# The second block's modulation: from TensorE in the delta rule to VectorE beside the first two perceptrons

## The reference, cut to what matters

```
def ada_params(cvec, w_ada, b_ada):
    return jnp.split(jax.nn.silu(cvec) @ w_ada + b_ada, N_ADA, axis=-1)
...
    for l in range(DEPTH_2):
        last = l == DEPTH_2 - 1
        sa, ca, ga, sm, cm, gm = ada_params(c_lat, w_ada[l], b_ada[l])
        sa_c, ca_c, ga_c, sm_c, cm_c, gm_c = ada_params(c_cx, w_ada[l], b_ada[l])
        ...
        h = modulate(rms_norm_2(x, g_mix[l]), sa, ca)
        hc = modulate(rms_norm_2(ctx, g_mix[l]), sa_c, ca_c)
```

## Time and profile before

| | us |
|---|---|
| median of 3 runs (2899.91 to 2905.57) | 2902.4 |
| the profiled execution, its own time | 2905.16 |
| its span, first to last instruction | 2903.4 |
| TensorE busy | 2716.3 (94%) |
| VectorE busy | 1439.0 (50%) |
| ScalarE busy | 887.6 (31%) |
| GpSimd busy | 88.5 (3%) |
| delta stage, about | 371 to 798 |
| first perceptron, start, about | 1020 |

### The profile page before, as it was taken

One profiled execution on the slowest core, in us unless ns is written; L12 is line 12 of the kernel. 1 busy time (PEld: TensorE's weight loads), 2 busy tenths in 40 slices (PEclk: granted clock), 3 DMA queues, 4 the chain that ended last, 5 costly groups with the idle time before them and its releaser, 6 DMA issues.

```text
span 2903.4 us, 48524 instructions
## 1 busy us (share of the span) xinstructions
PE 2716.3 (94%) x20932; PEld 2174.1 (75%) x20932; DVE 1439.0 (50%) x2470; ACT 887.6 (31%) x1508; POOL 88.5 (3%) x141
## 2 busy tenths in 40 slices
PE   6899988888899999999899899999999899899998
PEld 4677565667878788877777678888888776688876
DVE  3455555668853454434366654333334456544434
ACT  3344411100032333223345433222222345333322
POOL 0000011112200000000000000000000000000000
PEclk9999999999999999999999999999999999999999
DMA  6100545540023222221100212111210100232220
GB/s 255 58 30 5 198 169 199 220 169 3 3 89 123 87 87 91 111 89 60 53 30 30 87 34 83 59 58 59 72 74 30 40 30 30 116 115 88 88 87 29
DMA packets 17954, 242.43 MB, mean 83 GB/s; under 512 B 2032, under 2 KB 2192, under 8 KB 2896
## 3 DMA queue, kind: packets, MB, share of 16 engines
q1 hardware_dynamic: 16416, 231.94, 21.4%
q0 software_dynamic: 1328, 7.39, 0.7%
HBM read 237.23 MB, written 2.10 MB: 82 GB/s over the span
## 4 chain that ended last, share of the span: by engine, by line
PE 88%; DVE 7%; issue 2%; ACT 1%; DMA 1%; DVEq 0%; ACTq 0%; POOLq 0%
PE ps L333 54%; PE ps L1274 7%; PE ps L413 2%; PE ps L1847 2%; PE ps L2076 2%; PE ps L929 1%; PE ps L2104 1%; PE ps L362 1%; PE ps L2120 1%; PE ps L363 1%; PE ps L364 1%; PE ps L885 1%; PE ps L2122 1%; PE ps L2121 1%; DMA raw<-in_w_ada 1%
## 5 line engine op out<-in xcount | busy, mean ns | idle before, releaser
L333 PE MATMUL ps<-hh,ws 128*128 128x512 f32 x3216 | 751.7, 393 | 13.5 <-DVE hh L504 6.7
L333 PEld LDWEIGHTS ps<-hh,ws 128*128 128x128 f32 x3216 | 602.1, 188 | 147.3 <-issue 18.2
L324 DVE TENSOR_TENSOR ws<-raw,ws 128x1024 fp32r<-128x1024 f32 x295 | 360.3, 1224 | 196.2 <-ACT ws L316 196.1
L316 ACT ACTIVATE ws<-raw 128x1024 fp32r<-128x1024 f32 x295 | 309.1, 1050 | 476.0 <-PE ps L333 433.3
L333 PE MATMUL ps<-g,ws 128*128 128x512 f32 x1536 | 364.4, 395 | 0.0
L333 PEld LDWEIGHTS ps<-g,ws 128*128 128x128 f32 x1536 | 286.1, 188 | 67.2
L1274 PEld LDWEIGHTS ps<-ar 64*64 64x64 f32 x6656 | 213.9, 140 | 57.3 <-issue 37.6
L1274 PE MATMUL ps<-ar 64*64 64x64 f32 x6656 | 229.5, 226 | 21.9 <-issue 12.3
L1587 DVE SCALAR_TENSOR_TENSOR xT<-ps,mods,xT 128x512 f32<-128x512 f32 x120 | 90.1, 750 | 317.1 <-PE ps L333 307.6
L333 PE MATMUL ps<-gg,ws 128*128 128x512 f32 x960 | 226.1, 395 | 0.0
L333 PEld LDWEIGHTS ps<-gg,ws 128*128 128x128 f32 x960 | 180.2, 188 | 43.7
(11 more groups left out here) (338 smaller groups left out, 3337.5 us busy)
## 6 DMA issues: line engine op xcount, KB each, us to landing
raw<-in_w_ada SPq DMA_DIRECT2D x36, 2048.0 KB, 8.7
raw<-in_w_m SPq DMA_DIRECT2D x32, 2048.0 KB, 7.7
raw<-in_w_mlp SPq DMA_DIRECT2D x16, 2048.0 KB, 7.7
raw<-in_w_in SPq DMA_DIRECT2D x8, 2048.0 KB, 7.9
raw<-in_w_mg SPq DMA_DIRECT2D x8, 1536.0 KB, 6.7
raw<-in_w_out SPq DMA_DIRECT2D x6, 2048.0 KB, 7.8
raw<-in_w SPq DMA_DIRECT2D x5, 2048.0 KB, 7.7
xT<-in_xT POOLq DMA_DIRECT2D x1, 2048.0 KB, 16.2
```

Of the source, the lines that this page charges most:

```text
L316: e.activation(w_of(n)[0], pieces[n][2], ACT.Copy).then_inc(*hi(n))
L324: e.tensor_tensor(l, pieces[n][2], h.bitcast(F32), ALU.subtract).then_inc(*lo(n))
L333: m = e.matmul(o, a, b, start=n == 0, stop=n == 3 * kt - 1)
```

## The change

The 24 modulation blocks of the second block leave the delta stage, TensorE, and SP's queue; blocks 10 and 11 stay there. A new function `modulation` gives three programs that run beside a perceptron. The host lays silu's argument out as 1024 values (c, then c_ctx) on all 128 partitions, and the weights with output features on partitions. For output tile t (128 features) and vector j VectorE multiplies 128x1024 weights by the silu and sums along the row, with the bias as start value, in one `tensor_tensor_reduce`. Layer 0 has 96 such products beside m0, layer 1 64 beside m1 (the context's part of the last layer stops after tile 15). They are spread over the turns 9 to 59. Turns 0 to 3 have the four ScalarE steps of the silu over 128x2048, turns 3 and 4 VectorE's two. POOL's queue loads the weights: beside m0 24 times two tiles (1 MB) into two buffers, beside m1 48 times one tile (0.5 MB) into one buffer, which lies with the silu in a slot of `raw` that is held during m1 (`ada_slot`), so m1's own weights have two slots. Each product waits for its weights and for the product before it.

```diff
 
         UNIT_ADA = 6
-        adas = [(I["w_ada"], b, 0) for b in range(12)] + [(I["w_ada2_0"], b, 1) for b in range(12)] \
-            + [(I["w_ada2_1"], b, 2) for b in range(12)]
+        NADA = 12
...
         slot2, soft2 = [None, None], [None, None]
+        ada_slot = None
         for l in range(2):
             in_blocks(l, I[f"w_in2_{l}"])
             dense(f"o{l}0", I[f"w_out2_{l}"][0])
             let_go(f"att{l}")
             let_go(f"mix{l}")
             dense(f"o{l}1", I[f"w_out2_{l}"][1])
+            if l == 0:
+                ada_slot = hold("ada_slot")
             mlp_blocks(f"m{l + 1}", I[f"w_m1_{l}"], I[f"w_m2_{l}"])
+            if l == 0:
+                let_go("ada_slot")
 
         load_slot = {x[0]: x[1] for x in loads}
...
-            return 4 + UNIT_ADA + i // 8 if i % 8 == 7 and i // 8 < 32 - UNIT_ADA else None
+            return 4 + UNIT_ADA + i // 8 if i % 8 == 7 and i // 8 < NADA - 4 - UNIT_ADA else None
...
+        def modulation(l, at, n, at_weights, tiles_a_load):
+
+            cb = at[:, 0:2048]
+            u = at[:, 2048:4096]
+            junk = at[:, 2048:3072]
+            w = [at_weights[:, i * tiles_a_load * 1024:(i + 1) * tiles_a_load * 1024].rearrange(
+                "p (t f) -> p t f", t=tiles_a_load) for i in range(n)]
+            jobs = [(t, j) for t in range(48) for j in range(2 if l == 0 or t < 16 else 1)]
+            last_of = {t // tiles_a_load: (t, j) for t, j in jobs}
+            START, STOP = 9, 60
+            tag = ("silu_c", l)
+
+            def gpsimd(e):
+                e.dma_start(cb, I["c2"]).then_inc(*come["cb"](l, 16))
+                e.wait_ge(*dve[tag])
+                for i in range(48 // tiles_a_load):
+                    if i >= n:
+                        e.wait_ge(*dve["modulated", l, last_of[i - n]])
+                    e.dma_start(w[i % n], I["w_ada2"][l][:, i * tiles_a_load:(i + 1) * tiles_a_load, :]).then_inc(
+                        *wada_in[i % n]((l, i), 16))
+
+            def scalar(e):
+
+                return act_silu_c(e, tag, cb, u, [come["cb"][l]])
+
+            def vector(e):
+                for _ in range(3):
+                    yield
+                for _ in dve_silu_c(e, tag, cb, u, cb, [come["cb"][l]]):
+                    yield
+                for piece in range(5, 64):
+                    yield
+                    for n_, (t, j) in enumerate(jobs):
+                        if START + n_ * (STOP - START) // len(jobs) == piece:
+                            i = t // tiles_a_load
+                            e.wait_ge(*wada_in[i % n][l, i])
+                            e.wait_ge(*dve["modulated", l, jobs[n_ - 1]] if n_ else dve[tag])
+                            e.tensor_tensor_reduce(junk, w[i % n][:, t % tiles_a_load, :], cb[:, j * 1024:j * 1024 + 1024],
+                                                   1.0, Q2("bada", l)[:, t:t + 1], ALU.mult, ALU.add,
+                                                   mods[:, 1 + l, t, j:j + 1]).then_inc(*dve(("modulated", l, (t, j))))
+                            if n_ == len(jobs) - 1:
+                                dve.also(("mods", l))
+                                if l:
+                                    dve.also("ada_slot")
+
+            return gpsimd, scalar, vector
...
+                beside = aside[1](e) if aside else iter(())
                 for q in range(4):
                     for m in range(8):
+                        next(beside, None)
                         split_hi(e, start("u", q) + m + 2)
...
+                beside = aside[2](e) if aside else iter(())
                 for q in range(4):
                     for m in range(8):
+                        next(beside, None)
                         split_lo(e, start("u", q) + m + 2)
...
-        mlp0 = mlp_streams("m0", mod, [(0, hh, gg, xT, T, SQX, 7)])
+        mod_l0 = modulation(0, ar[:, 9216:13312], 2, ar[:, 13312:17408], 2)
+        mod_l1 = modulation(1, ada_slot, 1, ada_slot[:, 3072:4096], 1)
+        mlp0 = mlp_streams("m0", mod, [(0, hh, gg, xT, T, SQX, 7)], mod_l0)
+
+        def gpsimd_mlp0(e):
+            e.wait_ge(*acc["out", 7])
+            mod_l0[0](e)
...
-                if l == 0:
-                    e.wait_ge(*dve["mod", 35])
+                e.wait_ge(*dve["mods", l])
                 dve_gain(e, A1, md, 1, 0, Q2("gmix", l))
                 dve_gain(e, A1c, md, 1, 1, Q2("gmix", l))
                 dve_gain(e, A2, md, 4, 0, Q2("gmlp", l))
-                dve_gain(e, A2c, md, 4, 1, Q2("gmlp", l))
+                if not last:
+                    dve_gain(e, A2c, md, 4, 1, Q2("gmlp", l))
                 dve.also((l, "gains"))
...
                 meet(e, pool, (l, "attention"))
+                if l == 0:
+                    e.wait_ge(*acc[load_before["ada_slot"]])
+                    mod_l1[0](e)
...
+    A["w_ada2"] = x["w_ada_2"].reshape(2, 1024, 48, P).transpose(0, 3, 2, 1)
+    A["c2"] = np.broadcast_to(np.concatenate([x["c_2"][0], x["c_ctx_2"]])[None], (P, 2048))
```

More of the change, by code:

```diff
@@ L380, in build, with act_silu_c @@
         ada_row = ar[:, 12288:12800]
[L382 to L389 removed]
+        cvec = Q("c").rearrange("p (k j) -> p k j", j=2)
+        def act_silu_c(e, tag, c, u, waits):
+            for t in waits:
+                e.wait_ge(*t)
+            e.activation(u, c, ACT.Abs).then_inc(*act())
+            yield
@@ L390, in act_c @@
             e.wait_ge(*act.prev())
[L391 removed]
+            e.activation(u, u, ACT.Exp, scale=-1.0).then_inc(*act())
+            yield
             e.wait_ge(*act.prev())
[L393 to L403 removed]
+            e.activation(u, u, ACT.Ln, bias=1.0).then_inc(*act((tag, "u1")))
@@ new lines, in act_silu_c, with dve_silu_c @@
+            yield
+            e.wait_ge(*dve[tag, "u2"])
+            e.activation(u, u, ACT.Exp).then_inc(*act((tag, "u3")))
+        def dve_silu_c(e, tag, c, u, o, waits):
+            for t in waits:
+                e.wait_ge(*t)
+            e.wait_ge(*act[tag, "u1"])
+            e.scalar_tensor_tensor(u, c, 0.0, u, ALU.min, ALU.subtract).then_inc(*dve((tag, "u2")))
+            yield
+            e.wait_ge(*act[tag, "u3"])
+            e.tensor_tensor(o, c, u, ALU.mult).then_inc(*dve(tag))
```

71 lines of the change are left out of this document (29 added, 42 removed).

## The result

The changed kernel took 2817.4 us (the median of three runs, 2815.5 to 2822.8), the kernel before 2901.2 us (the median of four, 2899.3 to 2905.6) on the same chip. A fourth run of the changed kernel, at 7236 us, is left out as disturbed; with it the median is 2820.1. The ratio is 0.9713, with a 95% interval of 0.9691 to 0.9735: some 83 us less. The profiled execution took 2822.8 us (span 2821.1), 82.3 us less than the one of before. The forecast for the median was 2832 us, with a range of 2816 to 2862.

A forecast was written before the change was run, and what follows sets the result against it. TensorE, busy 94% of the span, was taken to bound the kernel. Terms -78.7 + 2.9 + 4 + 0.5 + 0.6 = -70.7 us took the profiled 2905.16 us to 2834.5, or 2832 us for the median; range 2816 to 2862.

The forecast's parts named there:

- step 6: Second perceptron, one weight slot less and 64 products: nine reload waits of about 6 us, hidden by 2 us; cost 0.6 us.
- Step 1: Delta stage: 24 modulation blocks leave TensorE's queue, saving 78.7 us, with bounds of 49 and 82.
- The bound of 2.03 us a block: Delta stage: lower price of a block, from s5, the quickest step with four blocks; 49 us for 24 blocks.
- the rival of the recurrence's own chain: Delta stage: TensorE waits for VectorE where blocks stood, a block worth only 2.03 us; 2861 us; chance 9 in 100.
- Step 2: Delta stage: the blocks' weight loads go, later loads up to the second block keep their slots; nothing gained or lost.
- Step 3: Start of the first perceptron: the 2048-wide silu delays the splits, TensorE waits near piece 5; cost 2.9 us.
- Step 4: First perceptron: 96 products at 1.4 us each on VectorE make it late in up pieces; cost 4 us.
- the 2.1 us of free lateness: First perceptron: VectorE may be 2.1 us late at a quarter's last hidden row before TensorE waits.
- Step 5: First perceptron: 24 weight loads of 1 MB on POOL's queue into two buffers; 0.5 us allowed in all.
- My rival of late weights: Both perceptrons: reloads meeting weight loads come later than VectorE's lead, some 25 us more; 2857 us; chance 10 in 100.
- The rule: VectorE products: scalar_tensor_tensor with two non-bf16 SBUF sources runs at half throughput, so a column costs twice the rows' 1.07 ns.
- the first rival: Perceptrons: products at half rate, 2.5 us each, make VectorE the first one's bound; +28 us, 2930 us; chance 7 in 100.

The follow-up runs named there:

- the two slowed reloads: Changed kernel with each weight tile beside the second perceptron loaded twice (2933.85 us), or reloaded behind a waited-for 64 KB load (2880.5 us).

## Why the prediction was right

The sign was right, and so was the mechanism but for step 6. The size was too small by 11.6 us: -70.7 forecast between profiles, -82.3 measured; 2832 us forecast for the median, 2817 measured (2820 over all four runs), at the lower end of the range. Of the 11.6 us, 2.9 come from the terms of the sum and 8.7 from stages for which it had no term. The gain of 83 us lies just above the forecast's 60 to 82; it stays in the range because that had 7 us more for a higher granted clock in the delta stage, and the extra lies elsewhere. That part is luck. Point by point:

*Step 1, the blocks: right.* The three terms were 40.4 (s1 to s3), 35.1 (s4 to s6) and 3.2 (s0), 78.7 in all; measured 38.2, 38.1 and 0.8, 77.1 in all. A step without latent work and without blocks takes 27.3 us (26.6 forecast), one of s4 to s6 28.7 (29.7 forecast from s7 to s11; the granted clock is 0.96 in s4 to s6 and 0.94 in s7 to s11). The 0.8 of s0 says little: its mark stands anywhere from 398 to 406 us in the profiles of the two kernels and their variants. A block among the quads takes 2.4 us of TensorE at the upper clock level (526.16 to 528.60 us in the kernel before) and up to 3.8 at the lower one; 3.3 us each were measured, TensorE's idle time included. The bound of 2.03 us a block was far off; 12 blocks less gave 35 to 49 us. With it falls the rival of the recurrence's own chain.

*Step 2, the loads of the delta stage: right.* Nothing waits for them anew; s7 to s11 is unchanged. In the kernel before none of the waits listed for s1 to s6 names a load either, so the blocks' loads are no rival for the cost of their work.

*Step 3, the silu: right.* 2.9 forecast, 3.4 measured by the two stages of 362.8 and 366.2 us. It is also where the forecast put it. The fourth silu instruction waits for VectorE's, and the split queued behind it comes late (ScalarE's timeline, then TensorE's):

```profile
968.60 1.92 ACT L402 ACTIVATE ar<-ar 128x2048 f32<-128x2048 f32 x1 [2.96 <-DVE ar L408]
970.41 1.04 ACT L321 ACTIVATE ws<-raw 128x1024 fp32r<-128x1024 f32 x1
```

```profile
963.70 6.51 PE L338 MATMUL ps<-hh,ws 128*128 128x512 f32 x28
972.81 3.45 PE L338 MATMUL ps<-hh,ws 128*128 128x512 f32 x14 [2.61 <-issue]
```

The silu placed eight pieces later costs nothing that shows: the first three down quarters take 44.96 us each there, as with nothing added. That kernel's 0.7 us (363.5 less 362.8) contain a pause of TensorE of 0.48 us in the last quarter.

*Step 4, the 96 products: mis-sized, 4 us forecast and 0.1 measured.* VectorE's timeline of an up piece:

```profile
1047.79 1.28 DVE L1667 CUSTOM_DVE_ANT_0 ar<-ar,par 128x1024 f32<-128x1024 f32 x1
...
1049.21 1.28 DVE L1667 CUSTOM_DVE_ANT_0 ar<-ar,par 128x1024 f32<-128x1024 f32 x1
1050.43 0.08 DVE L1667 DVE_READ_ACCUMULATOR2_ANT mods<- 128x1 f32 x1
1050.43 1.22 DVE L329 TENSOR_TENSOR ws<-raw,ws 128x1024 fp32r<-128x1024 f32 x1
...
1053.56 1.28 DVE L1667 CUSTOM_DVE_ANT_0 ar<-ar,par 128x1024 f32<-128x1024 f32 x1
```

The second product starts 1.42 us after the first, as assumed, but the split starts 1.22 us after the second, with its sum's read. Two products take 2.64 us of the queue, not 2.8, and the rest of the piece 3.13, not 3.31. The period is 5.77 us, so VectorE loses 0.33 us a piece to TensorE's 5.44, not 0.67. Over six pieces that is 2.0 us, and the 2.1 us of free lateness, which the forecast had right, just hold it. The last hidden row of the quarter starts at 1081.83 and ends at 1082.52; TensorE's next quarter starts at 1077.59 and wants it after 7/8 of a piece of 5.6, at 1082.5. That quarter lasted 45.15 us and the one before 44.96, as both do with the silu alone (VectorE's timeline, then TensorE's): 0.2 us lost. The idle of 1 to 2 us near piece 24 that the forecast named did not come.

```profile
1081.83 0.69 DVE L1739 TENSOR_TENSOR gg<-sq,gg 128x512 fp32r<-128x512 f32 x1 [0.70 <-ACT gg L1719]
```

```profile
989.25 44.96 PE L338 MATMUL ps<-gg,ws 128*128 128x512 f32 x192
...
1077.59 45.15 PE L338 MATMUL ps<-gg,ws 128*128 128x512 f32 x192
```

That nothing was lost is no proof of much room: three products in every piece cost 34.5 us in this stage, four in most pieces 95. Three beside the down pieces alone, with one or two beside the up pieces, cost 0.7 at most. So it is the up pieces that have no room for a third.

*Step 5, the loads beside the first perceptron: right*, 0.5 forecast; they land in 5.1 us and no wait for them shows.

*Step 6, the second perceptron: right in its number, wrong in its mechanism.* The forecast was 0.6 us from nine single waits of 6 us with 2 us of cover each. Measured: 547.0 us with and without the products, and VectorE's waits for the tiles (us in total, times, longest) are hidden, in 14 places:

```profile
DVE raw L1667 <- DMA raw<-in_w_ada: 46.0, 14, 5.2
```

But the cover is not 2 us per place. From tile 16 on one tile is used up in each 6.7 us, and the buffer's cycle of product, issue, load and landing must fit in that. In the changed kernel, where VectorE waits, two products stand 1986.98 - 1981.64 = 5.3 us apart (VectorE's timeline):

```profile
1981.64 1.28 DVE L1667 CUSTOM_DVE_ANT_0 raw<-raw,par 128x1024 f32<-128x1024 f32 x1
...
1986.98 1.28 DVE L1667 CUSTOM_DVE_ANT_0 raw<-raw,par 128x1024 f32<-128x1024 f32 x1 [4.05 <-DMA raw<-in_w_ada]
```

So the margin is about 1.3 us a tile, and beyond it a delay counts 32 times. A cycle of 7.85 us cost 58.5 us of the stage, 41 of them idle time of TensorE. My rival of late weights had the place right and priced the second perceptron's part at nine times 1 to 2 us; with late loads on the scale of the two slowed reloads it is several times that.

*The rule of the first rival.* The product takes 1281 ns for 1024 columns, 1.25 ns a column with all its fixed cost in it, beside 1.07 between two sizes of scalar_tensor_tensor and 1.05 of tensor_tensor in the earlier trace rows. Half of the throughput would have been 2.1 ns or more. The Trainium skill, Vector Engine (DVE) Microarchitecture Reference, section Points that are easy to get wrong, states that half for scalar_tensor_tensor with two non-bf16 SBUF sources; the trace disagrees for that instruction without a sum, and the measurement decides. The product is another instruction, with two such sources and a sum, and isn't halved either; scalar_tensor_tensor with a sum stands in no run here.

*What the sum lacked.* The measured terms are -77.1 + 3.4 + 0.1 + 0 + 0 = -73.6. The other 8.7 us of -82.3 have no work behind them. In the last layer's head it is 4.4, of which 3 are shown above to move with the granted clock. In the first perceptron it is 1.3 (364.1 before, 362.8 with nothing added). There the kernel before has a pause of 1.0 us at the start of the last quarter (TensorE's timeline), in both of its profiles; the kernel with half of the blocks and those without them don't have it:

```profile
1285.59 43.76 PE L333 MATMUL ps<-hh,ws 128*128 128x512 f32 x192 [1.00 <-DVE xT L1587]
```

In the second perceptron it is 1.6: from the second quarter on each quarter takes 134.8 us in the kernel before and 134.1 after, with TensorE busy throughout at a granted clock of 1.00, so neither a wait nor the clock explains it. The causes of both are open. The last 1.4 are small pieces. A single profile of before is no firm base at this size either: its second one is 6.9 us longer, 5.8 of them in s1 to s6, at a granted clock of 0.89 instead of 0.93 in s1 to s3. The same 12 blocks took 120.2 and 124.0 us in s1 to s3; TensorE's busy time for the same 2084 records rose from 103.1 to 106.1 us with the lower clock. Why the clock was lower there is open. The kernel with half of the blocks has eleven in s1 to s3 and took 115.6 us.

## What to carry to other kernels

Work that stands in the queue of the engine that bounds a stage costs at least its full length (here 2.4 us at the upper clock level, 3.3 measured), and the trace of before often holds the comparison, in steps with and without it. Work for a half idle engine must be counted per piece of the loop against the lateness that its consumer allows: here two products beside an up piece were free and three were not, while three beside a down piece were. A single reload buffer is judged by its cycle against the rate at which tiles are used up, not by the longest single wait; while the cycle fits in that interval a late tile costs nearly nothing, and once it doesn't every tile adds to the delay.
